# Router by ranks, squares summed by a product, and the first expert pair's rows selected on PE

## The chip, the core and the metric

The kernel runs on one core of a Trainium2 chip. The metric is device time in microseconds (us), the median over runs of one program. A run also gives a trace: what every engine did, how long, and what it waited for. Engines are PE (matmul), DVE (vector), ACT (activation), POOL and SP (here they only issue transfers); the data moves over 16 DMA engines.

## The reference

One step of a hybrid layer over 256 prompt tokens and 32 sample tokens, in float32. The stretch that matters here is the end of the layer: the residual stream, its norm, the router of the hierarchical mixture of experts, and the experts.

```python
h = x + mixed @ lw['w_o']
h = h + _hier_moe(_rmsnorm(h, lw['g_ffn']), lw)
...
g_idx = jnp.argmax(x @ w_grp + b_grp)                    # 1 group of 4
g_w   = softmax(g_logits)[g_idx]
top_v, top_i = lax.top_k(e_logits of that group, 2)      # 2 of its 4 experts
weights = g_w * softmax(top_v)
y = sum over experts of gate * (silu(x@w1) * (x@w3)) @ w2    # 16 experts, 2048 -> 512 -> 2048
```

Each of the 16 experts holds three matrices of 4 MB; all 201 MB are read once.

## The kernel before

**Stages.** Input projections, attention branches and merges run up to the product with `w_o`; then the router; then eight pairs of experts; then the last norm and the output. PE runs through all of it in program order, and so does each other engine; they meet at semaphores. There is no planner: the order is that of the code.

**The `w_o` loop** (PE L1107 to L1124). For each of 16 tiles `m` of 128 channels: a product of 16 matmuls into bank `m % 2` (L1113, waits for weight strips in a ring of four), then three transposes that bring tile `m` of the residual input `x` to channels-first (L1120), then `router(m - 1)` (L1088): logits of the tile before, accumulated in bank 2 (L1094), and its transposes to token rows (L1102, L1104). The residual input comes in four chunks (`x_chunk`, L1549) that ACT issues after a barrier of the engines (`phase_wait`), two at the start and two later; PE waits for a chunk by `xr_in`. A float32 matmul shows as two rows ("passes") in the trace, a transpose as one. ACT copies the transposed residual out of its bank (L1569), and DVE adds it to half the product (L2041), which gives `hTt`, tile `m` of h.

**The router** (DVE L2049 to L2128). ACT squares the token rows with a running sum (L1562), a product with a mask gathers the sample rows' sums over the four 32-row groups they are spread on (PE L1132), then mean, root, reciprocal, logits times scale plus bias (L2060). `first_max` (five short steps, L2069) is called three times: for the group, for the first and the second expert. From the one-hots come the assignment `AS`, its running counts per expert ("ranks", PE L1138 to L1141) and the gates. A token's rank is its slot (64 per expert). The largest count goes to `flag`, which each engine loads for a branch (`few_tokens`, L335); with at most 64 tokens per expert, as here, the engines take the branch described next.

**The pairs.** `pick(i)` (DVE L2162) builds a 0/1 matrix `sel` of tokens by 2x64 slots; `prepare(i)` (PE L1147) makes slot indices (L1151) and the transposed matrix (L1154) from it; `slots_of(i)` (DVE L2172) turns them into integers; POOL then gathers 128 rows of 8 KB of h by an indirect DMA from a copy in DRAM (L717) into `XGt`; PE transposes them (`gathered`, L1164) and DVE scales them into `XG` (`rows_in`, L2192). The up products of pair 0 and 7 run in eight steps (`up_fine`, L1183), each over one 2 MB slot of weights; the others in four steps of two slots (L1200). Then `down(i)`: transposes of the next pair's rows (`next_rows`, L1207, waits for its gather), transposes of the hidden layer (L1222), products with `w2` (L1233), and the scatter back to token rows (L1250). `prepare(i + 1)` stands early in the up products of pair `i`: in pair 0 after the second step (L1188).

**Weights.** Of 96 slots of 2 MB, nine fit on chip (`NSLOT`). Nine are loaded ahead; each later one is issued by SP when PE has finished with the slot's old content (L565: eight releases in the up products, two after the first half of `w2`, two after the second). So 87 fills follow the first release.

## Time and profile before

| | |
|---|---|
| median of 3 runs | 2096.85 us (2095.13 to 2097.07) |
| the profiled execution: time, and span of the trace | 2095.78 us, 2094.0 us |
| busy in the span: PE, DVE, ACT, POOL | 2019.7, 606.3, 257.6, 63.8 us |
| moved by DMA, mean rate | 404.31 MB, 193 GB/s |
| expert weights per slot | 2048 KB |

Times in rows are us from the start of the span. A matmul row's name ends with the tile (128*128) and the shape. Busy time says little here: PE is busy 96% of the span over stages with different limits. What counts is, stage by stage, what the last wait is for, and whether the DMA engines have work.

### The profile page before, as it was taken

Reading aid. Unit: us, or ns where it says so; the run is one execution under the profiler, and the core shown is the slowest. Engines: PE = TensorE matmul, PEld = TensorE weight load, DVE = VectorE, ACT = ScalarE, POOL = GpSimd, SP = SyncE. Lnnn points to the kernel's source line nnn. Section 1 sums busy time; section 2 is a strip of 40 time slices with the busy share of each in tenths; the row PEclk is TensorE's granted clock in tenths of the full one; section 3 lists DMA queues with packets and bytes.
Section 4 is the critical chain, followed back from the end, with each engine's and each line's share of the span. In section 5 each row is a group of like instructions: output and inputs, shape, how many; then the busy total and the mean of one; then the engine's idle time right before and its main releaser. Section 6 shows DMA issues by size and latency. Waiting matters only on the chain.

```text
span 2094.0 us, 26605 instructions
## 1 busy us (share of the span) xinstructions
PE 2019.7 (96%) x11213; PEld 1353.0 (65%) x11213; DVE 606.3 (29%) x1624; ACT 257.6 (12%) x619; POOL 63.8 (3%) x119
## 2 busy tenths in 40 slices
PE   7999999999999999999999999999996999989997
PEld 4767788777777777777777777777774333333332
DVE  3053222212212443534435345321003222121212
ACT  2121112122201010110101101000001000000002
POOL 0010000000000000000000000000000000000000
PEclk9999999999999999999999999999997999999999
DMA  9563434433234132431323313366433999999997
GB/s 300 93 194 122 134 125 149 158 129 119 86 121 148 59 125 73 135 114 54 125 92 116 125 42 123 119 219 223 153 130 131 422 428 426 428 427 427 428 423 277
DMA packets 196554, 404.31 MB, mean 193 GB/s; under 512 B 11632, under 2 KB 165968, under 8 KB 181328
## 3 DMA queue, kind: packets, MB, share of 16 engines
q1 hardware_dynamic: 187472, 379.37, 49.8%
q0 software_dynamic: 6304, 19.14, 3.3%
q10 hardware_dynamic: 2656, 4.06, 0.6%
q8 instruction: 90, 1.47, 0.3%
q14 instruction: 32, 0.26, 0.0%
HBM read 391.88 MB, written 10.67 MB: 192 GB/s over the span
## 4 chain that ended last, share of the span: by engine, by line
PE 88%; DMA 9%; DVE 1%; DVEq 1%; issue 0%; ACT 0%; SPq 0%; ACTq 0%
PE bank L766 21%; PE bank L970 19%; PE bank L972 6%; PE bank L1113 6%; PE bank L764 5%; PE bank L1200 5%; PE bank L1233 3%; PE bank L1080 3%; DMA Z<-in_w 3%; PE bank L1250 3%; DMA SC<-in_w 3%; PE bank L1183 2%; DMA ring<-in_w 2%; PE bank L1021 1%; PE bank L1015 1%; PE bank L743 1%
## 5 line engine op out<-in xcount | busy, mean ns | idle before, releaser
L766 PE MATMUL bank<-uT,ring 128*128 128x288 f32 (+2 forms) x1792 | 452.6, 409 | 0.6 <-DVE uT L1672 0.6
L970 PE MATMUL bank<-uT,ring 128*128 128x288 f32 x1536 | 408.1, 415 | 0.0
L766 PEld LDWEIGHTS bank<-uT,ring 128*128 128x128 f32 (+2 forms) x1792 | 332.1, 188 | 98.6 <-issue 7.8
L970 PEld LDWEIGHTS bank<-uT,ring 128*128 128x128 f32 x1536 | 283.6, 190 | 79.7 <-issue 3.1
L972 PE MATMUL bank<-Z,ring 128*128 128x288 f32 x512 | 140.5, 417 | 0.0
L1113 PE MATMUL bank<-SC,ring 128*128 128x288 f32 x512 | 128.4, 409 | 1.1 <-DVEq L355 1.1
L764 PE MATMUL bank<-ring,Z 128*128 128x256 f32 x512 | 117.4, 382 | 0.0
L1113 PEld LDWEIGHTS bank<-SC,ring 128*128 128x128 f32 x512 | 96.0, 190 | 29.6 <-DVEq L355 1.6
L1200 PE MATMUL bank<-ring,Z 128*64 128x512 f32 x352 | 104.5, 626 | 8.3 <-issue 8.3
L972 PEld LDWEIGHTS bank<-Z,ring 128*128 128x128 f32 x512 | 92.7, 189 | 25.6 <-issue 1.4
L764 PEld LDWEIGHTS bank<-ring,Z 128*128 128x128 f32 x512 | 95.4, 190 | 16.1 <-issue 3.7
L1522 ACT ACTIVATE Z<-bank 128x288 f32<-128x288 f32 x48 | 19.7, 411 | 589.5 <-PE bank L970 589.5
L1200 PE MATMUL bank<-Z 128*64 128x512 f32 x256 | 88.2, 609 | 4.1 <-issue 4.1
L2218 DVE TENSOR_TENSOR uT<-uT,bank 128x512 f32<-128x512 f32 x63 | 43.3, 688 | 115.3 <-PE bank L1250 115.3
L1200 PEld LDWEIGHTS bank<-ring,Z 128*64 128x64 f32 x352 | 32.9, 143 | 56.6 <-issue 56.5
L1200 PE MATMUL bank<-SC,Z 128*64 128x512 f32 x160 | 58.2, 608 | 5.6 <-issue 5.6
L1080 PE MATMUL bank<-Z,ring 128*128 128x288 f32 x256 | 62.3, 406 | 0.5 <-issue 0.5
L1080 PEld LDWEIGHTS bank<-Z,ring 128*128 128x128 f32 x256 | 48.6, 190 | 14.3 <-issue 1.0
L1250 PE MATMUL bank<-SC 128*128 128x512 f32 (+1 forms) x168 | 56.9, 601 | 0.0
L1200 PEld LDWEIGHTS bank<-Z 128*64 128x64 f32 x256 | 26.9, 140 | 41.2 <-issue 41.1
L1682 DVE TENSOR_TENSOR SC<-SC 128x287 f32<-128x287 f32 (+1 forms) x27 | 12.3, 457 | 138.5 <-ACT SC L1398 138.1
L2041 DVE SCALAR_TENSOR_TENSOR Z<-bank,Z 128x288 f32<-128x288 f32 x16 | 7.3, 457 | 141.1 <-ACT Z L1569 118.4
(408 smaller groups left out, 1931.2 us busy)
## 6 DMA issues: line engine op xcount, KB each, us to landing
ring<-in_w_in SPq DMA_DIRECT2D x102, 1024.0 KB, 7.8
ring<-in_w SPq DMA_DIRECT2D x40, 2048.0 KB, 31.4
Z<-in_w SPq DMA_DIRECT2D x31, 2048.0 KB, 30.4
SC<-in_w SPq DMA_DIRECT2D x21, 2048.0 KB, 29.1
ring<-in_w_mem_kv SPq DMA_DIRECT2D x16, 1024.0 KB, 7.7
ring<-in_w_o SPq DMA_DIRECT2D x16, 1024.0 KB, 7.7
ring<-in_p_b SPq DMA_DIRECT2D x8, 1024.0 KB, 5.3
ring<-in_p_m SPq DMA_DIRECT2D x8, 1024.0 KB, 8.0
```

Source lines behind the costliest of these rows:

```text
L743: ins = nc.tensor.transpose(bank[c % 8][:, t0:t0 + tn], X[0:tn, n, c * P:(c + 1) * P], ident[0:tn, 0:tn])
L764: ins = mm(bank[t][:, 0:STRIP], muT[:, c, P * t:P * t + P], rslot[q][:, c, :], start=c == 0, stop=c == KC - 1)
L766: ins = mm(bank[t][0:w, 0:T], rslot[q][:, c, w0:w0 + w], uT[:, c, :], start=c == 0, stop=c == KC - 1)
L970: ins = mm(b[:, 0:T], rslot[q][:, c, P * t:P * t + P], uT[:, c, :], start=c == 0, stop=c == last - 1)
L972: ins = mm(b[:, 0:T], rslot[q][:, k0 + c, P * t:P * t + P], Z[:, z0 + c, :], start=c == 0, stop=c == last - 1)
L1080: ins = mm(bank[n % 2][:, 0:T], wv[:, c, P * t:P * t + P], Z[:, Z_R + c, :], start=c == 0, stop=c == 7)
L1113: ins = mm(bank[m % 2][:, 0:T], rslot[(m // 2) % 4][:, c, P * (m % 2):P * (m % 2) + P], MX[:, c, :], start=c == 0, stop=c == KC - 1)
L1183: ins = mm(bank[2 + w][sides[x], :], XG[:, 4 * q + c, sides[x]], wv[:, x, c, :], start=q == 0 and c == 0, stop=q == 3 and c == 3)
L1200: ins = mm(bank[2 + w][sides[x], :], XG[:, 8 * h + c, sides[x]], wv[x][:, c, :], start=st < 2 and c == 0, stop=st >= 2 and c == 7)
L1233: ins = mm(bank[4 + b][sides[x], :], HS[:, 2 * h + c, sides[x]], wv[x][:, c, 512 * b:512 * b + 512], start=h == 0 and c == 0, stop=h == 1 ...
L1250: ins = mm(b[p0:p0 + tn, :], GP[:, i % 2, t0:t0 + tn], Yk[:, 512 * g:512 * g + 512], start=True, stop=True)
L2218: V.tensor_tensor(h, h, bank[SCB[n]][:, :], ALU.add).then_inc(s("sc_add"), 1)
```

## The change

In the `w_o` loop, the transposes of the residual tile (`residual`) stand one tile earlier: tile 0's ahead of the loop, tile `m + 1`'s behind the product of tile `m`. ACT squares each h tile channels-first (`tile_square`), DVE adds the squares of 15 tiles, and two products with a matrix of ones at the end put the sums of squares beside the logits, in rows 32 to 63 of bank 2. The sample tile's logits are brought to all four 32-row groups by four small products. DVE compares all logits of a group of four with each other at once; the number of larger ones is the rank within the group, from which `AS` follows. Softmax parts come after. PE gets small filler products (`keep_warm`). `pick` works in two steps over all slots instead of six. For pair 0 the rows are selected by products of h's token rows with `sel` (`own_rows`, 12 matmuls for each quarter, two quarters before and two within the up products) in place of the gather through DRAM; `prepare(0)` stands after the sixth up step and `prepare(1)` after the eighth.

```diff
-        lgT = cut(Z_t, 15104, T)[0:LOGITS, :]
+        lgT = cut(Z_t, 15104, T)[0:64, :]
+        h2sum = cut(Z_t, 12288, T)
+        h2one = cut(Z_t, 13952, T)
+        cmp_gt = cut(Z_t, 12800, 15, 16)
+        cmp_eq = cut(Z_t, 13040, 15, 16)
...
-            pload(NK_t[:, D + KC:D + KC + P + 3], a["const"][:, K_M32:NCALL], "nk_in")
+            pload(NK_t[:, D + KC:D + KC + P + 3], a["const"][:, K_M32:K_TOK + 3], "nk_in")
+            pload(TRI4, a["const"][:, K_TRI4:NCALL], "nk_in")
...
-                for i in range(EXPERTS // 2):
+                for i in range(1, EXPERTS // 2):
                     pool.wait_ge(s("idx_ev"), i + 1)
-                    if i:
+                    if i > 1:
                         pool.wait_ge(s("xgt_mm"), 4 * i)
...
                 mm(bank[2][0:LOGITS, 0:T], wr[:, m, :], h, start=m == 0, stop=m == KC - 1)
+                if m == KC - 1:
+                    pe.wait_ge(s("h2_add"), KC - 1)
+                    mm(bank[2][32:64, 0:T], ones[:, 0:32], h2sum, start=True, stop=False)
+                    pe.wait_ge(s("sq_done"), 14 + KC)
+                    mm(bank[2][32:64, 0:T], ones[:, 0:32], h2one, start=False, stop=True).then_inc(s("rt_mm"), 1)
...
+            def residual(m):
+
+                g = m // 4
+                pe.wait_ge(xr_in[g], 64)
+                if m >= 2:
+                    pe.wait_ge(s("xts"), m - 1)
+                for tt, (t0, tn) in enumerate(TOK):
+                    ins = nc.tensor.transpose(bank[4 + m % 2][:, t0:t0 + tn], XRC[g % 2][0:tn, tt, P * (m % 4):P * (m % 4) + P], ident[0:tn, 0:tn])
+                ins.then_inc(s("res_mm"), 1)
+
+            residual(0)
...
                 for c in range(KC):
                     ins = mm(bank[m % 2][:, 0:T], rslot[(m // 2) % 4][:, c, P * (m % 2):P * (m % 2) + P], MX[:, c, :], start=c == 0, stop=c == KC - 1)
                 ins.then_inc(s("wo_mm"), 1)
-                g = m // 4
-                pe.wait_ge(xr_in[g], 64)
-                if m >= 2:
-                    pe.wait_ge(s("xts"), m - 1)
-                for tt, (t0, tn) in enumerate(TOK):
-                    ins = nc.tensor.transpose(bank[4 + m % 2][:, t0:t0 + tn], XRC[g % 2][0:tn, tt, P * (m % 4):P * (m % 4) + P], ident[0:tn, 0:tn])
-                ins.then_inc(s("res_mm"), 1)
+                if m + 1 < KC:
+                    residual(m + 1)
...
-            pe.wait_ge(s("lg_ev"), 1)
-            pe.wait_ge(s("xts"), KC)
+            def keep_warm(n):
+
+                for _ in range(n):
+                    mm(bank[0][:, 0:P], ident, ident, start=True, stop=True)
+
+            pe.wait_ge(s("lg_ev"), 2)
+            for tt in range(2):
+                t0, tn = TOK[tt]
+                nc.tensor.transpose(bank[4][:, 64 * tt:64 * tt + 64], lgT[:, t0:t0 + tn], ident[0:64, 0:64])
+            for g in range(4):
+                ins = mm(bank[4][TS * g:TS * g + TS, P:P + 64], lgT[:, TP:T], ident[0:64, 0:64], start=True, stop=True)
+            ins.then_inc(s("rt_mm"), 1)
+            keep_warm(14)
+
+            pe.wait_ge(s("rt_a"), 1)
+            tri = CON[:, K_TRI:K_TRI + P]
+            for tt in range(3):
...
             for tt, (t0, tn) in enumerate(TOK):
-                ins = nc.tensor.transpose(bank[4][0:tn, 32 * tt:32 * tt + LOGITS], lgT[:, t0:t0 + tn], ident[0:LOGITS, 0:LOGITS])
-            pe.wait_ge(s("nk_in"), 96)
-            pe.wait_ge(s("sq_done"), 23)
-            mm(bank[5][:, 0:1], M32, ssq[:, 2, 0:1], start=True, stop=True).then_inc(s("rt_mm"), 1)
...
+                ins = mm(bank[1][:, 0:16], ones[0:tn, :], AS[0:tn, tt, :], start=tt == 0, stop=tt == 2)
             ins.then_inc(s("rank_mm"), 1)
+            keep_warm(4)
+
+            def own_rows(q):
+
+                for c in range(4):
+                    out = bank[4 + q % 2][:, P * c:P * c + P]
+                    for tt in range(2):
+                        mm(out, H[:, tt, 512 * q + c:512 * q + 512:4], sel[:, tt, :], start=tt == 0, stop=False)
+                    gs = slice(TS * q, TS * q + TS)
+                    ins = mm(out, H2[gs, c:512:4], sel[gs, 2, :], start=False, stop=True)
+                ins.then_inc(s("xgt_mm"), 1)
+
+            pe.wait_ge(s("tok_ev"), 9)
+            pe.wait_ge(s("sel_done"), 1)
+            own_rows(0)
+            own_rows(1)
             few = few_tokens(pe)
...
-                        if st == 1 and i + 1 < NPAIR:
-                            pe.wait_ge(s("xg_ev"), 4 * i + 4)
-                            prepare(i + 1)
+                        if i == 0 and st in (1, 3):
+                            pe.wait_ge(s("xg_ev"), st // 2 + 1)
+                            own_rows(2 + st // 2)
+                        if i == 0 and st == 5:
+                            prepare(0)
+                        if i == 0 and st == 7:
+                            pe.wait_ge(s("idx_ev"), 1)
+                            pe.wait_ge(s("gp_ev"), 1)
+                            prepare(1)
...
-                            pe.wait_ge(s("gath"), 16 * i + 32)
+                            pe.wait_ge(s("gath"), 16 * i + 16)
...
-                prepare(0)
-                pe.wait_ge(s("idx_ev"), 1)
-                pe.wait_ge(s("gp_ev"), 1)
-                pe.wait_ge(s("gath"), 16)
-                gathered(0, range(4))
...
+            def tile_square(m):
+
+                act.wait_ge(s("h_tile"), m + 1)
+                if m >= 2:
+                    act.wait_ge(s("h2_add"), m)
+                A(h2one if m else h2sum, hTt[:, m % 2, :], ACT.Square).then_inc(s("sq_done"), 1)
...
+                if m:
+                    tile_square(m - 1)
+            A(dummy[:, 0:1], vec["eps"][:, 0:1], ACT.Sqrt)
+            tile_square(KC - 1)
+            act.wait_ge(s("rt_mm"), 1)
+            A(lgT[32:64, :], bank[2][32:64, 0:T], ACT.Copy).then_inc(s("lg_ev"), 1)
             act.wait_ge(s("tail_mm"), KC)
-            A(lgT, bank[2][0:LOGITS, 0:T], ACT.Copy).then_inc(s("lg_ev"), 1)
-            for n in (3, 7, 8):
-                token_squares(False, n)
+            A(H[:, 0, 1536:2048], bank[3][:, :], ACT.Copy).then_inc(s("tok_ev"), 1)
             act.wait_ge(s("mean_sq"), 3)
             A(rst[:, 0:3], rsm[:, 0:3], ACT.Sqrt).then_inc(s("root"), 1)
+            A(H[:, 1, 1536:2048], bank[6][:, :], ACT.Copy).then_inc(s("tok_ev"), 1)
+            A(H2, bank[7][:, :], ACT.Copy).then_inc(s("tok_ev"), 1)
             A(dummy[:, 1:2], vec["eps"][:, 0:1], ACT.Exp)
...
+                if 2 <= m < KC:
+                    dve.wait_ge(s("sq_done"), 14 + m)
+                    V.tensor_tensor(h2sum, h2sum, h2one, ALU.add).then_inc(s("h2_add"), 1)
+                elif m == 1:
+                    dve.wait_ge(s("sq_done"), 15)
+                    dve.sem_inc(s("h2_add"), 1)
...
+            V.tensor_copy(lgT[0:LOGITS, :], bank[2][0:LOGITS, 0:T]).then_inc(s("lg_ev"), 1)
+            dve.wait_ge(s("rt_mm"), 2)
+            b4 = bank[4][:, 0:192].rearrange("p (t n) -> p t n", t=3)
+            V.tensor_scalar(rsm[:, 0:3], b4[:, :, 32:33].rearrange("p t a -> p (t a)"), 1.0 / D, EPS, ALU.mult, ALU.add).then_inc(s("mean_sq"), 1)
+            for tt in range(3):
+                V.scalar_tensor_tensor(lgt[:, tt, :], b4[:, tt, 0:LOGITS], rsm[:, tt:tt + 1], bias, ALU.mult, ALU.add)
+            dr()
+            fours = lgt.rearrange("p t (g x) -> p (t g) x", x=4)
+            rank, oh, top, dif, num = cut(RT, 60, 3, LOGITS), cut(RT, 120, 3, 4), cut(RT, 132, 15, 1), cut(RT, 148, 3, LOGITS), cut(RT, 208, 3, EXPERTS)
+            den, sumg = cut(RT, 368, 3, 1), cut(RT, 372, 3, 1)
+            other, own = fours.unsqueeze(2).to_broadcast([P, 15, 4, 4]), fours.unsqueeze(3).to_broadcast([P, 15, 4, 4])
+            gt4, eq4 = (b.rearrange("p g (x y) -> p g x y", x=4) for b in (cmp_gt, cmp_eq))
+            V.tensor_tensor(eq4, other, own, ALU.is_equal)
+            V.tensor_tensor(gt4, other, own, ALU.is_gt)
+            dr()
+            V.tensor_tensor(cmp_eq, cmp_eq, TRI4.unsqueeze(1).to_broadcast([P, 15, 16]), ALU.mult)
+            dr()
+            V.tensor_tensor(cmp_gt, cmp_gt, cmp_eq, ALU.add)
+            dr()
+            V.reduce_sum(rank.rearrange("p t n -> p (t n)"), cmp_gt.rearrange("p g (x y) -> p (g x) y", x=4), AX.X)
+            dr()
+            V.tensor_scalar(oh, rank[:, :, 0:4], 0.0, None, ALU.is_equal)
+            dr()
+            V.scalar_tensor_tensor(AS.rearrange("p t (g x) -> p t g x", x=4), rank[:, :, 4:LOGITS].rearrange("p t (g x) -> p t g x", x=4), 1.5,
+                                   oh.unsqueeze(3).to_broadcast([P, 3, 4, 4]), ALU.is_lt, ALU.mult)
+            dr()
+            dve.sem_inc(s("rt_a"), 1)
+            V.reduce_max(top.rearrange("p g a -> p (g a)"), fours, AX.X)
+            dr()
+            V.tensor_tensor(dif.rearrange("p t (g x) -> p (t g) x", x=4), fours, top.to_broadcast([P, 15, 4]), ALU.subtract)
+            dr()
+            dve.sem_inc(s("rt_a"), 1)
...
+            def pick(i):
+
+                one_hot = sel.rearrange("p t (x n) -> p t x n", x=2)
+                iota = CON[:, K_IOTA:K_IOTA + SLOTS].unsqueeze(1).unsqueeze(1).to_broadcast([P, 3, 2, SLOTS])
+                V.tensor_tensor(one_hot, iota, RK[:, :, 2 * i:2 * i + 2].unsqueeze(3).to_broadcast([P, 3, 2, SLOTS]), ALU.is_equal)
+                dr()
+                V.tensor_tensor(one_hot, one_hot, AS[:, :, 2 * i:2 * i + 2].unsqueeze(3).to_broadcast([P, 3, 2, SLOTS]), ALU.mult)
+                dr()
+                dve.sem_inc(s("sel_done"), 1)
+
+            def own_in(q):
+
+                dve.wait_ge(s("xgt_mm"), q + 1)
+                V.tensor_tensor(XG[:, 4 * q:4 * q + 4, :], bank[4 + q % 2][:, :].rearrange("p (a b) -> p a b", a=4),
+                                GV2[:, 4 * q:4 * q + 4].unsqueeze(2).to_broadcast([P, 4, P]), ALU.mult).then_inc(s("xg_ev"), 1)
+
+            dve.wait_ge(s("rank_mm"), 1)
+            V.tensor_copy(RK, bank[2][:, 0:48].rearrange("p (t n) -> p t n", t=3))
+            dr()
+            pick(0)
+            dve.wait_ge(s("rank_mm"), 2)
+            V.reduce_max(CNT[:, 0:1], bank[1][:, 0:16], AX.X)
+            dr()
+            V.tensor_copy(flag[:, :], CNT[:, 0:1]).then_inc(s("flag_done"), 1)
+
...
+            own_in(0)
+            own_in(1)
...
-                    if i:
-                        dve.wait_ge(s("gath"), 16 * i)
+                    if i > 1:
+                        dve.wait_ge(s("gath"), 16 * i - 16)
                     rs = slot_rs[:, i % 2:i % 2 + 1]
                     V.tensor_copy(slot_tok[:, :], bank[0][:, 0:1])
...
-                pick(0)
+                own_in(2)
+                own_in(3)
                 slots_of(0)
                 dve.wait_ge(s("gp_mm"), 1)
                 pick(1)
-                rows_in(0)
                 for i in range(EXPERTS // 2):
                     last = i + 1 == EXPERTS // 2```

On PE, at the head of the `w_o` loop (L1113 is the product of a tile, L1120 the residual's transposes, `xr_in0` the arrival of chunk 0, `phase_done` the barrier; L1080 belongs to the stage ahead), the order before:

```order
L1080 MATMUL bank<-Z,ring 128x288 x7
L1113 MATMUL bank<-SC,ring 128x288 [waits ring_full0,phase_done]
L1113 MATMUL bank<-SC,ring 128x288 x15
L1120 MATMUL bank<-CON,NK 128x128 [waits xr_in0]
L1120 MATMUL bank<-CON,NK 128x128
L1120 MATMUL bank<-CON,NK 128x32
L1113 MATMUL bank<-SC,ring 128x288 x16
```

and of the changed kernel, where the lines are L1137 (product) and L1127 (transposes):

```order
L1088 MATMUL bank<-Z,ring 128x288 x7
L1127 MATMUL bank<-CON,NK 128x128 [waits xr_in0,phase_done]
L1127 MATMUL bank<-CON,NK 128x128
L1127 MATMUL bank<-CON,NK 128x32
L1137 MATMUL bank<-SC,ring 128x288 [waits ring_full0]
L1137 MATMUL bank<-SC,ring 128x288 x15
L1127 MATMUL bank<-CON,NK 128x128 [waits xr_in0]
```

The wait for chunk 0 moved from behind the first product to ahead of it.

On PE in pair 0's up products (L1183), the order before, from the second step on (L1151 and L1154 are `prepare(1)`; `moe_full` is the arrival of a weight slot):

```order
L1183 MATMUL bank<-Z 64x512 [waits moe_full1]
L1183 MATMUL bank<-Z 64x512 x7
L1151 MATMUL bank<-Z,SC 128x18 [waits sel_done,xg_ev]
L1151 MATMUL bank<-Z,SC 128x18 x2
L1154 MATMUL bank<-CON,SC 128x128 x2
L1154 MATMUL bank<-CON,SC 128x32
L1183 MATMUL bank<-Z 64x512 [waits xg_ev,moe_full2]
```

and of the changed kernel, from the eighth step (L1230 is the up product, L1198 and L1201 `prepare(1)`, L1211 the transposes of pair 1's gathered rows):

```order
L1230 MATMUL bank<-ring,Z 64x512 [waits moe_full7]
L1230 MATMUL bank<-ring,Z 64x512 x7
L1198 MATMUL bank<-Z,SC 128x18 [waits sel_done,gp_ev,idx_ev]
L1198 MATMUL bank<-Z,SC 128x18 x2
L1201 MATMUL bank<-CON,SC 128x128 x2
L1201 MATMUL bank<-CON,SC 128x32
L1211 MATMUL bank<-CON,NK 128x128 [waits gath,gp_ev,idx_ev]
```

`prepare(1)`, on which pair 1's gather depends, moved from six steps ahead of the transposes of its rows to right in front of them.

## Rows read from the trace of the kernel before

**Rows 1.** Windows, two pairs: stretch, length, busy per engine, PEclk, DMA share, GB/s.

```profile
1617.50:1671.40 53.90, 53.90 (x248) 20.30 (x247) 12.35 (x26) 4.08 (x7) 1.00 (x1) 1.00 0.92 386
...
1941.00:1995.00 54.00, 48.77 (x211) 17.77 (x211) 8.95 (x17) 3.92 (x7) 0.94 (x1) 0.98 1.01 428
```

**Rows 2.** Chain that ended last, late pairs: start, length, what it was.

```profile
1980.66 30.49 DMA Z<-in_w
...
2056.48 16.65 DMA ring<-in_w
```

**Rows 3.** Timeline, head of the `w_o` loop: start, length, instruction, [idle before, releaser].

```profile
1394.61 35.81 PE L1080 MATMUL bank<-Z,ring 128*128 128x288 f32 x147
...
1431.52 0.47 ACTq L1552 DMA_DIRECT2D NK<-in_x_prompt  x1
...
1431.55 8.03 PE L1113 MATMUL bank<-SC,ring 128*128 128x288 f32 x32 [1.13 <-DVEq L355]
...
1440.77 0.61 PE L1120 MATMUL bank<-CON,NK 128*128 128x128 f32 x3 [1.20 <-DMA NK<-in_x_sample]
...
1441.32 8.03 PE L1113 MATMUL bank<-SC,ring 128*128 128x288 f32 x32
```

**Rows 4.** Windows around the router (PEclk is the third number from the end).

```profile
1588.00:1590.00 2.00, 0.01 (x1) 0.00 (x0) 1.28 (x3) 1.82 (x5) 1.18 (x2) 0.95 1.00 426
1590.00:1592.00 2.00, 0.56 (x2) 0.50 (x2) 0.55 (x3) 0.75 (x4) 1.55 (x4) 0.50 1.20 492
...
1600.00:1602.00 2.00, 1.97 (x12) 1.75 (x11) 0.05 (x1) 0.00 (x0) 0.00 (x0) 0.50 0.00 0
...
1614.00:1616.00 2.00, 2.00 (x9) 1.67 (x10) 0.72 (x2) 0.00 (x0) 0.00 (x0) 0.50 0.00 0
1616.00:1617.50 1.50, 1.50 (x10) 1.26 (x10) 1.13 (x2) 0.00 (x0) 0.00 (x0) 0.63 0.00 0
```

**Rows 5.** Chain from the last `w_o` products to the first expert product.

```profile
1584.39 0.39 PE bank L1120 x3
...
1598.47 0.61 PE bank L1139 x2
...
1600.47 1.51 PE bank L1141 x6
...
1602.68 0.55 DVEq L338
...
1603.69 0.32 DVE SC L2167
...
1607.74 6.11 DMA NK<-h_rows,slot_tok
...
1617.56 7.02 PE bank L1183 x32
```

**Rows 6.** Lines by form, 1430 to 1672: count, busy us, mean ns, idle before.

```profile
L2030 DVE TENSOR_TENSOR Z<-Z,VEC 128x320 f32<-128x320 f32 x1 | 0.5, 491 | 0.2 <-DVEq L355 0.2
...
L2073 DVE TENSOR_TENSOR Z<-Z 128x12 f32<-128x12 f32 x3 | 0.5, 171 | 0.2
```

**Rows 7.** Chain, pair 0 into pair 1.

```profile
1624.57 0.87 PE bank L1151 x6
...
1646.74 1.09 PE bank L1164 x8
...
1649.50 13.88 PE bank L1233 x64
1663.38 8.06 PE bank L1250 x24
```

**Rows 8.** Timeline of POOL and SP, pair 0: pair 1's gather, two weight fills.

```profile
1626.41 1.00 POOL L717 DMA_INDIRECT NK<-h_rows,slot_tok  x1 [17.65 <-DVEq L2185]
...
1656.56 1.19 SPq L534 DMA_DIRECT2D SC<-in_w  x2
```

**Rows 9.** View of tile NK, its gathers: from issue to landing.

```profile
DMA to landing us min/median/max: 6.1/13.3/13.5
```

More of the change, by code:

```diff
@@ L64 @@
 K_M32, K_TOK = 1344, 1472
-NCALL = 1475
+K_TRI4 = 1475
+NCALL = 1491
 BW = 640
@@ L1135, in _ @@
-            tri = CON[:, K_TRI:K_TRI + P]
-            for tt, (t0, tn) in enumerate(TOK):
-                for u in range(tt):
-                    mm(bank[6][0:tn, 16 * tt:16 * tt + 16], ones[:, 0:tn], AS[:, u, :], start=u == 0, stop=False)
-                mm(bank[6][0:tn, 16 * tt:16 * tt + 16], tri[0:tn, 0:tn], AS[0:tn, tt, :], start=tt == 0, stop=True)
-            for tt, (t0, tn) in enumerate(TOK):
-                ins = mm(bank[6][:, 48:64], ones[0:tn, :], AS[0:tn, tt, :], start=tt == 0, stop=tt == 2)
@@ new lines, in _ @@
+            ins.then_inc(s("rt_mm"), 1)
[3 more added lines that the diff above has]
+            for tt in range(3):
+                out = bank[2][:, 16 * tt:16 * tt + 16]
+                for u in range(tt):
+                    mm(out, ones, AS[:, u, :], start=u == 0, stop=False)
+                if tt < 2:
+                    mm(out, tri, AS[:, tt, :], start=tt == 0, stop=True)
+            for g in range(4):
+                gs = slice(TS * g, TS * g + TS)
+                ins = mm(bank[2][gs, 32:48], tri[0:TS, 0:TS], AS[0:TS, 2, :], start=False, stop=True)
@@ L2041, in _ @@
                 V.scalar_tensor_tensor(hTt[:, m % 2, :], bank[m % 2][:, 0:T], 0.5, xTs[:, m % 2, :], ALU.mult, ALU.add).then_inc(s("h_tile"), 1)
-                g = (m if m == KC - 1 else m - 1) // 4
-                if m == KC - 1 or (m and m % 4 == 0):
+                if 2 <= m < KC:
[4 more added lines that the diff above has]
+                    dve.sem_inc(s("h2_add"), 1)
+                g = (m - 1) // 4
+                if m and m % 4 == 0:
                     dve.wait_ge(s("tail_mm"), 4 * g + 4)
@@ L2056, in _ @@
             dr()
-            b4 = bank[4][:, 0:96].rearrange("p (t n) -> p t n", t=3)
             bias = VEC[:, N_VEC_IN - 24:N_VEC_IN - 4]
-            for tt, (t0, tn) in enumerate(TOK):
-                V.scalar_tensor_tensor(lgt[0:tn, tt, :], b4[0:tn, tt, 0:LOGITS], rsm[0:tn, tt:tt + 1], bias[0:tn, :], ALU.mult, ALU.add)
+            for tt in range(3):
+                V.scalar_tensor_tensor(lgt[:, tt, :], b4[:, tt, 0:LOGITS], rsm[:, tt:tt + 1], bias, ALU.mult, ALU.add)
+            dr()
@@ L2082, in _ @@
-            gl = lgt[:, :, 0:4]
-            first_max(oh, gl, gm)
-            V.tensor_tensor(ge, gl, gm.to_broadcast([P, 3, 4]), ALU.subtract)
-            el = lgt[:, :, 4:20]
-            for t in range(3):
-                V.tensor_tensor(big[:, t, :].rearrange("p (g x) -> p g x", g=4), el[:, t, :].rearrange("p (g x) -> p g x", g=4),
-                                oh[:, t, :].unsqueeze(2).to_broadcast([P, 4, 4]), ALU.mult)
-            dr()
-            V.reduce_sum(ei, big.rearrange("p t (g x) -> p t x g", g=4), AX.X)
@@ L2091, in _ @@
-            dr()
-            first_max(oh1, ei, m1)
-            V.scalar_tensor_tensor(e2, oh1, TAKEN, ei, ALU.mult, ALU.add)
-            dr()
-            first_max(oh2, e2, m2_)
-            V.tensor_tensor(m2_, m2_, m1, ALU.subtract)
-            dr()
-            dve.sem_inc(s("rt_a"), 1)
-            V.tensor_tensor(e2, oh1, oh2, ALU.add)
-            dr()
-            for t in range(3):
-                V.tensor_tensor(AS[:, t, :].rearrange("p (g x) -> p g x", g=4), oh[:, t, :].unsqueeze(2).to_broadcast([P, 4, 4]),
-                                e2[:, t, :].unsqueeze(1).to_broadcast([P, 4, 4]), ALU.mult)
@@ L2128, in _ @@
+            dr()
+            V.reciprocal(den, den)
+            dr()
+            V.tensor_tensor(RI[:, :, 2:18], num, den.to_broadcast([P, 3, EXPERTS]), ALU.mult)
+            dr()
+            own_in(0)
+            own_in(1)
             few = few_tokens(dve)
             def out_norm(tt):
-                dve.wait_ge(s("sq_done"), (30, 31, 32)[tt])
+                dve.wait_ge(s("sq_done"), (37, 38, 39)[tt])
                 if tt < 2:
```

105 lines of the change are left out of this document (29 added, 76 removed).

## The prediction, made before the changed kernel was run

> **What bounds the kernel now.** I read the end first. In the chain that ended last, the late pairs are waits for weights, up to the last one, which ends at 2073.1 [rows 2]. The windows by pair say why: 386 GB/s in the first pair's window, then 421 to 428, with a DMA share of 1.01, in each of the seven that follow up to 2049 (one stands here), while PE has gaps [rows 1]. By amount: 87 fills of 2.10 MB, seven gathers of 1.05 MB and some 0.8 MB of gains make 191 MB, at 428 GB/s 446 us, which is nearly all of the time between the first release of a slot (one up step after the first expert product, near 1621) and 2073. So from there on DMA sets the end: what starts the first release earlier is gained in full, what leaves the DMA engines without work later is lost in full. Ahead of that, PE's own order sets the time: the `w_o` loop, then a chain of short steps of 33.2 us, from the last `w_o` product's end at 1584.39 to the first expert product at 1617.56 [rows 5].
>
> So I price three things: the moved transposes ahead of the loop, the shorter chain, and what the new order in pair 0 does to the fills.
>
> **The `w_o` loop: +8.6 us, and +1.5 for the clock.** Before, PE starts the first product at 1431.55, and only its transposes wait for the residual's chunk 0, which lands at 1440.77, 9.2 us after ACT issued it; 8.03 us of product hide that, 1.20 us do not [rows 3]. Now the transposes stand first, with that wait, and the first product has to follow at 1441.32, where before the second one started. From there on the loop holds one product more (8.03) and, at the end of the last product, one group of transposes more (0.54): +8.57. Nothing gives it back, since PE is dense through the loop. The landing does not move: ACT issues behind the same barrier. PE is then idle for 10.3 us (1430.42 to 1440.77). In the router PE had nothing to do from 1588, and the granted clock was 0.50 (1.2 GHz) from 1590 on; when dense work came back at 1613.98, it was still 0.50 until 1616 and came to 1.00 near 1617.1, that is 3.1 us at half rate [rows 4]. The same here costs half of that, 1.5. Extra work in the loop (one square on ACT, one add on DVE per tile, under 0.5 us each) hides behind 9.6 us of PE per tile.
>
> **The chain: 33.2 becomes 20.0, -13.2 us.** Counted from the end of the last `w_o` product:
> - PE: `router(14)` 1.1, the last tile's logits 0.5, two products of squares with 288 columns at four passes of 0.25 (a product of 32 passes took 8.03 [rows 3]) 1.0: 2.6. The squares of tile 15 (DVE 0.5, ACT 0.4, DVE 0.5) are ready by 1.6. Transposes of tile 15 0.7, ten small passes for the logits 0.9: 4.2.
> - Mean, root, reciprocal with their hops 0.85, three scale-and-bias steps 0.55: 5.6.
> - DVE's steps have 240 elements now. 12 cost 171 ns and 320 cost 491 [rows 6], so 1.04 ns each and 408 ns for 240; with 0.07 of drain five of them, the first two overlapping, take 2.3, two small ones 0.5: `AS` at 8.4. Before it came at 14.1 (1598.47, [rows 5]).
> - Ranks: 18 passes. At full clock a pass with a 128-column weight load took 0.136 (1.09 for 8 [rows 7]): 2.4, to 10.8. Copy 0.25 and two `pick` steps of 384 elements at 0.56 and 0.07: 12.3.
> - `own_rows` 0 and 1: 24 passes each, at 0.136 to 0.145 (0.87 for 6 of L1151 [rows 7]) 3.4 each: 19.1. I count 0.9 for loading `flag` and the branch; DVE needed 1.0 (1602.68 to 1603.69 [rows 5]), and PE may hide all of it behind queued products. The first step starts at 20.0.
>
> What disappears is the selection on DVE, the gather with 6.11 us, and its 16 transposes at half clock. The scaling by `own_in` (0.7) lies beside `own_rows(1)`. This needs full clock all the way; the filler products cover the longest wait (4.2 to 8.4).
>
> **Pair 0: +18.2 us.** With t = 0 at the first up product, a step takes 3.51 (7.02 for two [rows 5]). `own_rows` 2 and 3 stand behind the second and fourth, `prepare(0)` (1.4) behind the sixth, so slots come free at 3.5, 7.0, 13.9, 17.4, 24.3, 27.9, 32.8 and 36.3. A fill flows 1.1 after its release and for 4.91 (2.10 MB at 428 GB/s): two gaps of 0.6, and the eight fills are through at 45.1, with pair 1's gather (2.5 of its own) at 47.5. But the gather is issued late: `prepare(1)` comes after the eighth step, its index product ends at 37.2 (0.87 [rows 7]), and POOL issues 1.0 later (1625.44 to 1626.41 [rows 7, 8]), at 38.2. Landing took 6.1 with nothing else moving and 13.3 with full queues [rows 9]; the queues are full at first and empty at the end, so I take 11.5: 49.7. Right behind `prepare(1)` PE stands at the transposes that wait for it, and behind them all of `down(0)`. Before, from these transposes to the next release it took 9.8 (1646.74 to 1656.56 [rows 7, 8]); 12 us of idle PE add 1.5 for the clock. So the next release is at 61.0 and flows at 62.1: 14.6 without work since 47.5. That release gives two slots (9.8), 6.9 later there are two more, and the next only after the scatter and a step, at 61.0 + 6.9 + 8.1 + 7.0 = 83.0: the DMA has run out at 81.7, 2.4 more. Later PE is ahead again. Sum 1.2 + 14.6 + 2.4 = 18.2. Before, `prepare(1)` ran at 1624.57 and its gather had 20 us of cover: the rows were there at 1646.74 with no wait.
>
> The Trainium skill (DMA: Bandwidth & Descriptors, section Queues, rings and completion order) says that each DMA engine takes turns between the queues that have work, a packet at a time. With even turns the gather would land some 8.6 after issue (an estimate: 1.05 MB at half of 428 GB/s, and the 3.65 that its 6.1 leaves over), and the sum would be 2.9 lower; the measured 13.3 says it gets about a quarter, so the measurement stands.
>
> **The sum.** 8.6 + 1.5 - 13.2 + 18.2 = +15.1 on the profiled execution's 2095.78: 2110.9, say 2111. That execution lies 1.1 below the median shown, well inside what I can tell. The bounds: `own_rows` passes between 0.11 (no weight load to wait for, 0.25 x 128/288) and 0.25 (half clock, 1.51 for 6 [rows 5]); flag 0 to 1.0; the gather 6.1 to 13.5 (-5.4, +2.0); the clock terms 0 to 1.5 each.
>
> **Rivals.**
> - *The clock falls in the router.* The rank products have 16 columns. In the trace PE was busy with such products for 1.97 of 2 us and stayed at 0.50 [rows 4]; if they count as little, the clock falls after the fillers too. Then 18 passes cost 2.2 more and 48 of `own_rows` 5: 2118. Against it: the fillers are 128 columns wide, and no gap exceeds 1 us. The Trainium skill (TensorE: Matmul & The Clock Gate, Part 1) says that sustained time, not the number of matmuls, releases the half rate; by that the forecast stands, and the row of 1600 doesn't bear it out.
> - *The gather lands early*, because the fills in front run out: 6.1 as in the quiet router. The wait shrinks by 5.4: 2105.5.
> - *The shortfall is made good* (the other side). If the fills were not at their ceiling, PE's stall in pair 0 would leave slots to be caught up with, and only the first three terms stay: 8.6 + 1.5 - 13.2 = -3.1, 2092.7, not slower. It decides if the rate after pair 0 exceeds some 445 GB/s. One 2 us window shows 492 [rows 4]; against it stand the flat 428 and the share of 1.01.
>
> **Numbers.** Forecast 0.56 (2106 to 2116), clock 0.16, early gather 0.17, made good 0.11. About 0.2% (4 us) is what a measurement here can tell from no change. The last case lies around that bound: 0.04 faster, 0.07 the same; the rest, 0.89, is slower. The range 2101 to 2121 leaves out that case and the far end of the clock's.
>
> **What would show it.** Right: PE idle some 10 us ahead of the first residual transposes near 1441, the last `w_o` product ending near 1594; the first up product 20 us behind it at clock 1.00; a PE wait of about 12 us for the gather between pair 0's up and down, with a hole in GB/s right behind it; then 428 to the end, the last landing near 2088. Wrong: a first up product before 1605 (chunk 0 earlier), no wait at the gather, a clock of 0.50 in `own_rows`, or windows above 440 GB/s after pair 0.

## The result, and the profile after

The changed kernel takes 2133.01 us (median of 5 runs, 2132.14 to 2133.99) against 2095.74 for the kernel before on the same chip: a ratio of 1.0178 [1.0164, 1.0192]. It is slower, as forecast, but by 37 us instead of 15; 2133 lies outside the range of 2101 to 2121. The profiled execution took 2132.14 with a span of 2130.3, 36.3 more than before.

I follow the prediction's three places in order. The head of the `w_o` loop, from the chain of the changed kernel that ended last (start, length, what it was):

```profile
1429.94 0.47 ACTq L1601
1430.44 7.82 DMA NK<-in_x_sample
1438.40 0.90 PE bank L1127 x3
1439.30 10.10 PE bank L1137 x32
```

The transposes (L1127) now wait for the residual's chunk, and the first product (L1137) takes 10.10 us where one at full clock takes 8.03 [rows 3]. The last `w_o` product ends at 1592.80, before at 1584.39. The barrier was 1.6 us earlier in this execution, so the stage is 10.0 longer. The sum is as predicted (+10.1), its parts are not: PE got the chunk 8.5 us after ACT's first issue instead of 9.2, and half clock cost some 2.4 (0.3 in the transposes, 2.1 in the product) instead of 1.5.

The chain from there to the first expert product, by the same view:

```profile
1592.80 0.59 PE bank L1102 x2
...
1600.30 0.39 PE bank L1166 x2
...
1603.72 1.03 PE bank L1181 x4
1604.75 0.76 PE bank L1183 x2
1605.52 1.23 PE bank L1181 x4
1606.75 0.76 PE bank L1183 x2
...
1619.47 5.67 PE bank L1230 x13
```

The ranks start 7.5 us behind the last product (predicted 8.4) and `own_rows` (L1181, L1183) 10.9 behind it (12.3): the router by ranks is faster than I reckoned. Then `own_rows` 0 and 1 take 15.75 together, 7.9 each, where 3.4 each were predicted: six passes take 1.79 to 1.99 us, or 0.30 to 0.33 a pass, not 0.136 to 0.145. The first expert product comes 26.7 behind the last `w_o` product; predicted were 20.0, before it was 33.2 [rows 5].

Pair 0, by the chain, up to pair 1's first step:

```profile
1629.00 1.13 PE bank L1181 x4
1630.13 0.66 PE bank L1183 x2
...
1636.36 9.62 PE bank L1230 x32
1645.98 1.13 PE bank L1181 x4
...
1653.33 9.67 PE bank L1230 x32
...
1671.43 0.89 PE bank L1198 x6
...
1673.27 11.50 DMA NK<-h_rows,slot_tok
1684.77 0.14 issue
1684.91 1.94 PE bank L1211 x8
...
2092.52 17.01 DMA ring<-in_w
```

`own_rows` 2 and 3 cost 7.36 each, and two up steps behind each take 9.62 and 9.67 where two took 7.02 [rows 5]. So `prepare(1)` (L1198) starts 52.0 behind the first up product, 15.7 later than the 36.3 that I put. Its gather lands 11.50 after POOL issued it, the 11.5 taken.

Windows of the changed kernel around `own_rows` and through pair 0 (length, busy time of PE, PEld, DVE, ACT and POOL; the last three numbers are PEclk, DMA share and GB/s; the windows of 5 us first, then those by stage):

```profile
1600.00:1605.00 5.00, 4.70 (x37) 4.37 (x38) 3.41 (x16) 1.74 (x3) 0.11 (x1) 0.90 0.98 378
1605.00:1610.00 5.00, 5.00 (x16) 3.88 (x16) 0.06 (x1) 0.00 (x0) 0.00 (x0) 0.50 0.36 143
1610.00:1615.00 5.00, 5.00 (x17) 3.88 (x16) 0.69 (x1) 0.00 (x0) 0.00 (x0) 0.50 0.00 0
1615.00:1620.00 5.00, 5.00 (x16) 3.58 (x17) 0.49 (x1) 0.00 (x0) 0.00 (x0) 0.50 0.02 3
...
1636.00:1643.00 7.00, 7.00 (x22) 2.15 (x23) 0.69 (x1) 0.00 (x0) 0.00 (x0) 0.60 0.18 75
1643.00:1653.00 10.00, 10.00 (x38) 6.85 (x34) 0.00 (x0) 0.00 (x0) 0.00 (x0) 0.94 0.96 369
1653.00:1660.00 7.00, 7.00 (x22) 2.17 (x23) 0.69 (x1) 0.00 (x0) 0.00 (x0) 0.60 0.18 75
...
1685.00:1697.50 12.50, 12.50 (x58) 6.79 (x60) 2.77 (x4) 0.60 (x1) 0.00 (x0) 0.83 0.06 12
```

The clock falls to 0.50 (1.2 GHz) and stays there while PE counts as busy all the time. (A busy PE here is one with a matmul in flight, and a product is longer in flight when its weights load longer: at least 392 ns in L1181, 275 in the same line with columns side by side, in e1_contig below.) Each slow `own_rows` also opens a hole in the fills (75 GB/s) that the prediction's 0.6 us gaps don't have; the hole at the gather (12 GB/s) is the one predicted. From 1760 on there is no more to catch up with: the later pairs run at 422 to 428, before at 421 to 428 (428 in [rows 1]), and the last weights land at 2109.5, where 2088 was forecast.

### The profile page after: what moved, and what is told of

Same layout as the page of the kernel before. It is cut to its first block, busy times and chain, and to the rows that moved or that the text cites. A ratio compares the mean times of both kernels' runs of the same rounds, so it can differ in the third digit from the quotient of the medians.

```text
span 2130.3 us, 26820 instructions
## 1 busy us (share of the span) xinstructions
PE 2059.3 (97%) x11344; PEld 1381.7 (65%) x11344; DVE 606.3 (28%) x1579; ACT 259.1 (12%) x619; POOL 64.8 (3%) x119
## 4 chain that ended last, share of the span: by engine, by line
PE 90%; DMA 7%; DVE 1%; issue 1%; DVEq 0%; SPq 0%; ACT 0%; ACTq 0%
PE bank L774 20%; PE bank L978 19%; PE bank L980 6%; PE bank L1137 6%; PE bank L1253 6%; PE bank L772 5%; DMA Z<-in_w 5%; PE bank L1286 4%; PE bank L1088 3%; PE bank L1230 3%; PE bank L1303 2%; PE bank L1029 1%; PE bank L1023 1%; PE bank L1181 1%; DMA ring<-in_w 1%
## 5 line engine op out<-in xcount | busy, mean ns | idle before, releaser
L1137 PE MATMUL bank<-SC,ring 128*128 128x288 f32 x512 | 130.6, 414 | 0.0
L1137 PEld LDWEIGHTS bank<-SC,ring 128*128 128x128 f32 x512 | 97.5, 193 | 28.7 <-issue 2.8
L1088 PE MATMUL bank<-Z,ring 128*128 128x288 f32 x256 | 62.3, 407 | 0.5 <-issue 0.5
L1088 PEld LDWEIGHTS bank<-Z,ring 128*128 128x128 f32 x256 | 48.6, 190 | 14.2 <-issue 1.0
```

Source lines behind the costliest of these rows:

```text
L1088: ins = mm(bank[n % 2][:, 0:T], wv[:, c, P * t:P * t + P], Z[:, Z_R + c, :], start=c == 0, stop=c == 7)
L1137: ins = mm(bank[m % 2][:, 0:T], rslot[(m // 2) % 4][:, c, P * (m % 2):P * (m % 2) + P], MX[:, c, :], start=c == 0, stop=c == KC - 1)
```

## Experiments

My theory after the two traces: `own_rows` is slow because its stationary columns lie 4 apart, and that slowness moves everything in pair 0. The rival: the clock falls in the thin router, and `own_rows` is slow for that reason alone. All edits are to the changed kernel unless another is named. The kernel before took 2096.1 to 2096.4 in these sessions.

**Columns side by side (e1_contig).**

```diff
-  mm(out, H[:, tt, 512 * q + c:512 * q + 512:4], ...)
+  mm(out, H[:, tt, 512 * q + P * c:512 * q + P * c + P], ...)   # the 32-row product alike
```

> The changed kernel, but own_rows takes its stationary columns side by side (step 1) and not every fourth one (step 4). The channels of pair 0's rows are then in another order than its weights, so pair 0's contribution isn't the reference's; amount and order of the work are the same. Theory A (the weight load with a column step of 4 is what makes a pass of own_rows last 0.28 to 0.31 us, and the slow passes let PE's clock fall): passes of 0.13 to 0.15, one own_rows 3.3 us in place of 7.4 to 7.9, clock 1.00 through pair 0's up steps, first up product 9 us earlier, first release 12 us earlier, holes in the fills behind the second and fourth step gone (each under 1 us): 2133 falls by 22 to 27, to 2106 to 2111. Rival B (a real float32 product with changing weights costs 0.28 whatever the step, or the 32-row group does): own_rows stays at 7 to 8 us, the time at 2133 within 2. Rival C (the clock falls by itself, since the products of own_rows count as little work): passes 0.14 at full clock but 0.25 soon after, up steps still at half rate, gain 8 to 12: 2121 to 2125.

Pair 0's channels don't match its weights here; the work is the same. 2116.92 (2113.7 to 2119.1), ratio 1.0093 [1.0076, 1.0109], 16.1 faster than the changed kernel, where theory A has 22 to 27. The weight loads of L1181 by line, after and then here (ns: min, median, max):

```profile
L1181 PEld LDWEIGHTS bank<-SC,uT x64: 307/329/331, 1603.5 to 1651.9; 128*128 128x128 f32 x64
```

```profile
L1181 PEld LDWEIGHTS bank<-SC,uT x64: 186/192/338, 1603.4 to 1641.2; 128*128 128x128 f32 x64
```

Its chain, the first of `own_rows(0)`, then two up steps and the start of `own_rows(2)`:

```profile
1603.71 0.74 PE bank L1181 x4
...
1618.28 8.28 PE bank L1230 x32
1626.56 0.64 PE bank L1181 x4
1627.20 0.41 PE bank L1183 x2
```

At full clock one `own_rows` takes 4.2. But the clock still falls at 1604, so `own_rows` 0 and 1 still take 7.1 and 7.5. The step is the larger part, not the whole.

**`prepare` earlier (e2_prep).** `own_rows(2)` and `(3)` stand behind the first and second up step, `prepare(0)` and `prepare(1)` behind the third and fourth.

```diff
-  if i == 0 and st in (1, 3): ... own_rows(2 + st // 2)
-  if i == 0 and st == 5: prepare(0)
-  if i == 0 and st == 7: ... prepare(1)
+  if i == 0 and st in (0, 1): ... own_rows(2 + st)
+  if i == 0 and st == 2: prepare(0)
+  if i == 0 and st == 3: ... prepare(1)
```

> The changed kernel, with own_rows 2 and 3 behind the first and second up step of pair 0, prepare(0) behind the third and prepare(1) behind the fourth (they stood behind the second, fourth, sixth and eighth). Theory A (the gather of pair 1 is issued too late, PE waits 12 us for it and the DMA engines then have nothing to do for 14 to 16): no wait at the transposes of pair 1's rows, the hole before the first release of pair 0's down goes, the time falls by 14 to 18: 2115 to 2119. Rival (the fills have slack that is used later, so the wait costs little): under 4 us, 2129 to 2133.

2121.01 (2120.2 to 2121.99), ratio 1.0116 [1.0099, 1.0133], 12.0 faster: less than expected. The gather now has cover (PE waits 0.2 for it instead of 12.1). From the first up product to the first product of `down(0)` it is 56.2 instead of 69.9, so 13.8 of the 14 to 18 are there; in the profiled execution the last `w_o` product ended 2.2 later than in the changed kernel. Each single step between two `own_rows` runs at half clock in part (5.9 to 6.2 instead of 3.5), but all eight together take 35.8 in both kernels, so this is not what is missing.

**Residual order as before (e3_res).** `residual(0)` behind the first `w_o` product again, tile 1's right after it.

```diff
-  residual(0)
   for m in range(KC):
       ... product m
+      if m == 0: residual(0)
       if m + 1 < KC: residual(m + 1)
```

> The changed kernel, with the transposes of residual tile 0 behind the first product of w_o again (tile 1 follows at once, the others stay one tile ahead). Theory A (the first product no longer covers the arrival of the residual's chunk 0): the wait of 9.6 falls to 1 to 2, the first product runs at full clock, everything behind comes 10 us earlier: 2121 to 2125. Rival (the fills that are loaded ahead end later and take the gain back): 2131 to 2134.

2123.10 (2121.3 to 2124.95), ratio 1.0129 [1.0112, 1.0146], 9.9 faster, as theory A has it. This is about the head's term, 8.6 + 1.5.

**All three (e4_all)**, with pair 0's weights loaded so that channels fit contiguous columns (the computation is whole again).

```diff
+  if i == 0: return a[...][0:2, 512 * q:512 * q + 512, :].rearrange("e (c p) n -> p e c n", c=4)
   (and the three edits above)
```

> All three edits in one kernel, with the computation whole: pair 0's up weights are loaded in the matching order of channels (runs of 2 KB in place of 8 KB, two transfers for each slot) and scaled by the gain vector in that order. Theory A, if the three parts add up (10 + 24 + 16): 2080 to 2086, faster than both kernels; the first up product some 15 us earlier than in the kernel before. Rival (the parts share one shortfall of the fills, and the sum is smaller): 2092 to 2105.

2095.10 (2088.14 to 2100.68, 10 runs), ratio 0.9996 [0.9982, 1.001]. The parts add: 16.1 + 12.0 + 9.9 = 38.0, measured 37.9. (That close is luck: counted from the kernel before of each session they are 16.8, 12.7 and 10.6, and 38.6 measured.) The 2080 to 2086 are missed because two of the three parts are smaller than put. `own_rows` 0 and 1 are still at half clock. The runs spread over 12 us, and those with the higher mean clock are the faster ones (2088.14 at 0.992, 2100.68 at 0.986).

**Denser filler (e5_dense)** on that kernel.

```diff
-  mm(bank[0][:, 0:P], ident, ident, ...)       # keep_warm(14), keep_warm(4)
+  mm(bank[0][:, :], ident, CON[:, 0:512], ...) # keep_warm(9), keep_warm(4)
```

> e4_all with denser filler: each filler product moves 512 columns (an estimate from the up steps' 0.228 us per such pass: 0.46 us a product) instead of 128, 9 ahead of the ranks (about 4.1 us, up to when AS is ready) and 4 behind them. In e4_all the granted clock fell to .50 at the end of the second filler and the first two own_rows took 7.4 us each instead of 4.2, the first two up steps 4.5 instead of 3.65. Theory (the idle and thin work before own_rows lets the clock fall; dense filler keeps it): clock 1.00 through the ranks, own_rows 0 and 1 at 4.2 each, first up product about 6.5 us earlier than in e4_all, 2086 to 2089 us, and runs that spread less than e4_all's 2088 to 2101. Rival (the clock falls there whatever runs on PE, as a rest after the dense w_o loop): own_rows still 7.4, 2093 to 2098.

2095.91 (2094.28 to 2096.82), ratio 0.9998 [0.9989, 1.0007]. The clock stays at 1.00 and `own_rows` take 4.2 each, but the filler is too long: the timeline has

```profile
1588.72 7.99 PE L1151 MATMUL bank<-CON 128*128 128x512 f32 x18
```

0.89 a product, twice what I reckoned from up steps, whose stationary side has 64 columns and whose two experts' products run side by side (16 passes of 0.59 each in 3.58). What the clock gave, the filler took. This filler does two things at once: its products are wider, and it also closes the 0.8 us for which PE stands idle ahead of the ranks in the changed kernel. Which of the two holds the clock no run here shows.

**Column step within one `own_rows` (e6_steps).** Its four products read columns 1, 2, 4 and 8 apart (the 32-row ones at most 4).

```diff
-  H[:, tt, 512 * q + c:512 * q + 512:4]
+  H[:, tt, at:at + P * by:by]   # by = 1, 2, 4, 8 for c = 0..3 in own_rows 2, 3
```

> after, but in own_rows 2 and 3 the four products of a tile read their stationary columns 1, 2, 4 and 8 apart (so pair 0's rows are wrong channels; own_rows 0 and 1 as in after). At one clock, side by side: theory (the weight load is what the step makes slow): step 1 as in e1_contig, 0.64 us for the 4 passes of the two 128-row products, step 4 as in after, 1.13; step 2 between them or at one of the two, step 8 (128-row products only, the 32-row product stays at 4) 1.13 or more; loads of 190 ns at step 1, over 300 at step 4. Rival (the step matters only by way of the clock): all four alike within 0.1 us.

One run (2128.09). `own_rows(2)` by the timeline, a 128-row and a 32-row row for each product, all at clock 1.00:

```profile
1629.06 0.71 PE L1184 MATMUL bank<-SC,uT 128*128 128x128 f32 x4
1629.70 0.48 PE L1186 MATMUL bank<-SC,uT 32*128 32x128 f32 x2
1630.12 0.74 PE L1184 MATMUL bank<-SC,uT 128*128 128x128 f32 x4
1630.78 0.50 PE L1186 MATMUL bank<-SC,uT 32*128 32x128 f32 x2
1631.21 1.20 PE L1184 MATMUL bank<-SC,uT 128*128 128x128 f32 x4
1632.34 0.73 PE L1186 MATMUL bank<-SC,uT 32*128 32x128 f32 x2
1633.00 1.22 PE L1184 MATMUL bank<-SC,uT 128*128 128x128 f32 x4
```

Steps of 1 and 2 cost the same (0.71, 0.74), 4 and 8 cost the same (1.20, 1.22), and `own_rows(3)` repeats all four: an edge between 8 and 16 bytes, not a price that grows. The Trainium skill (SBUF — State Buffer, section Door 1: The DMA port swizzle) says that SBUF is read in lines of 16 bytes and that two hits in a line are needed to hide its latency. The edge of these products agrees. Its figure that a stride of 4 float32 is still free does not: 4 apart cost 1.7 times as much here. This rule I had not weighed, and it speaks against the change.

**The router alone (e7_router).** No `own_rows`: pair 0's rows are gathered as before, `prepare(0)` follows the gates, eight up steps stand with nothing between but `prepare(1)` behind the second.

```diff
-  own_rows(0); own_rows(1)
+  prepare(0); pe.wait_ge(s("gath"), 16); gathered(0, range(4))
-  for i in range(1, EXPERTS // 2):   # POOL
+  for i in range(EXPERTS // 2):
```

> The change without own_rows: router by ranks, squares by the product, whole sample tile, residual order as in after; pair 0's rows are gathered as in before (prepare(0) once the gates are done, gather, transposes, then eight up steps without anything between, prepare(1) behind step 2). Theory (the router's half of the change saves 12.5 us of the chain after w_o, and the order in the w_o loop costs 10; everything after the first up step is as before): selection and gates ready 12.4 us after the last w_o product instead of 20.8, from there to the first up product 12.3 as in before, so first up 1617 and 2094 to 2096 us. Rival (the shorter chain meets the gather with rows not yet written or fills still on the queues, so the wait at the gather grows): 2098 to 2103.

2100.67 (2098.68 to 2103.87), ratio 1.0024 [1.0013, 1.0034]: the rival. Its chain:

```profile
1599.74 1.50 POOL h_rows L717 x3
1601.24 8.22 DMA h_rows<-uT
...
1611.13 5.89 DMA NK<-h_rows,slot_tok
...
1621.03 7.47 PE bank L1216 x32
```

The gather no longer waits for the selection but for h's last token rows, which are written to DRAM beside the prefetch of weights and land 8.2 us after POOL's issue, 15 behind the last product. In the kernel before the slower selection hid that. So the faster router alone gives less than the 12.5 expected as long as the rows go through DRAM (5.6 by the next experiment). `own_rows` reads them in SBUF and has no such wait.

**The router alone, residual order as before (e8_router_res).**

```diff
   (the edits of the router alone and of the residual order)
```

> e7_router with residual(0) behind the first w_o product, as in e3_res. Theory: the two parts add, first up about 1606.5, everything behind it 10 to 11 us earlier than in before: 2084 to 2087 us, the best so far. Rival (the gather now meets the prefetch of pair 0's weights, which in before ends about 1598, and lands later): 2088 to 2094.

2090.48 (2088.72 to 2091.44, 9 runs), ratio 0.9974 [0.9964, 0.9984]: 0.3% faster than the kernel before, short of the 2084 to 2087 for the same wait (h's last rows land 8.04 after their issue; the gather itself takes 5.99). The two parts add (10.2 between this kernel and the last).

**Less of the dense filler (e9_dense2)**, on the kernel with all three edits.

```diff
-  keep_warm(9) ... keep_warm(4)
+  keep_warm(5) ... keep_warm(1)
```

> e5_dense with fewer filler products: 5 ahead of the ranks and 1 behind them instead of 9 and 4. e5_dense showed a 512-column product at 0.89 us (18 passes, 7.99 us), twice what was reckoned with, so its filler ended 3.7 us after AS was ready and then 2.5 us after the selection. Theory (e5_dense kept the clock and lost the same time to too much filler): the clock stays at 1.00 with 4.4 and 0.9 us of it, own_rows 4.2 each, first up product 6 us earlier than e5_dense's 1610.6, 2088 to 2091 us. Rival (that little filler doesn't hold the clock through the ranks and the wait for the selection): own_rows 7.4 each, 2094 to 2097.

2090.59 (2087.98 to 2092.76, 8 runs), ratio 0.9971 [0.9961, 0.9982]. It beats both kernels, the one before by 0.3%, the changed one by 42 us. The first up product starts at 1605.7 by its chain, 11.9 earlier than before; some 8 of that are given back in the profiled execution, about what `own_rows` 2 and 3 (4.2 each) put between the releases, though no run separates this. It is level with e8_router_res (2090.48), which gathers pair 0's rows through DRAM: with all these edits the way over `own_rows` comes out the same as the gather.

**The filler alone (e10_after_dense)**, on the changed kernel.

```diff
   (the dense filler, keep_warm(5) and keep_warm(1); columns still 4 apart)
```

> after with that filler alone (5 and 1 products of 512 columns), columns still 4 apart. Theory A (the clock falls because of the thin stretch between w_o and own_rows): own_rows 0 and 1 at 7.4 each instead of 7.9 and up steps 1 and 2 in 7.0 instead of 9.5, 2129 to 2131 us. Theory B (own_rows with columns 4 apart lets the clock fall by itself, as own_rows 2 and 3 of after do): clock down within own_rows 0 or 1, first two up steps still over 9 us, 2131 to 2134.

2133.08 (2131.49 to 2134.51), ratio 1.0177 [1.0162, 1.0193]: no gain, theory B (its first two up steps take 8.2 though, not over 9). Its windows:

```profile
1605.00:1610.00 5.00, 5.00 (x17) 3.92 (x17) 1.81 (x9) 0.00 (x0) 0.00 (x0) 1.00 0.80 289
1610.00:1615.00 5.00, 5.00 (x17) 3.88 (x16) 0.69 (x1) 0.00 (x0) 0.00 (x0) 0.51 0.00 0
```

The clock holds into `own_rows(0)` and then falls, with PE busy for 5.00 of 5. So with columns 4 apart it falls in `own_rows` itself, though it came through the filler and the ranks; the next experiment differs in the column step alone.

**Contiguous columns and the filler (e11_contig_dense)**, which is what the prediction assumed.

```diff
   (the first edit and the dense filler, 5 and 1)
```

> e1_contig with that filler (pair 0's channels don't match its weights, as there): both conditions that the prediction took for own_rows, a pass at the price of a transpose and full clock. If the failed term is the whole of the miss, it must come out near the predicted 2111: own_rows 4.2 each (predicted 3.4), first up 6 to 7 us earlier than in e1_contig, 2109 to 2112 us. Rival (something else in pair 0 that the prediction left out): 2114 or more.

2112.10 (2110.47 to 2114.17), ratio 1.0078 [1.0063, 1.0093]; the prediction's time was 2111. The same windows:

```profile
1605.00:1610.00 5.00, 5.00 (x30) 3.82 (x29) 0.92 (x3) 0.00 (x0) 0.00 (x0) 1.00 0.38 152
1610.00:1615.00 5.00, 5.00 (x27) 2.68 (x28) 0.69 (x1) 0.00 (x0) 0.00 (x0) 1.00 0.01 3
```

All four `own_rows` run at clock 1.00 and take 4.2 each, not the 3.4 predicted. That is 3.2 more in all, and the chain ahead of them is some 2 faster than put, so the forecast's sum comes to about 2112. The four kernels make a table of two by two: with columns 4 apart the filler gives nothing (2133.0, 2133.1), with contiguous ones 4.8 (2116.9, 2112.1; runs of one kernel spread over up to 5). `own_rows` 0 and 1 need both: they take 7.9 each in the changed kernel, 7.1 and 7.5 with the step alone mended, 7.4 and 8.0 with the filler alone, 4.2 with both.

## Why the prediction was wrong

The direction and three of its steps hold.
- *The `w_o` loop:* +10.1 predicted, +10.0 in the trace, 9.9 by the experiment that undoes it. The mechanism is right; that the sum fits so well is luck, since the chunk came 0.8 sooner and half clock cost 0.9 more than put.
- *The chain up to the selection:* 12.3 predicted, 10.9 measured, and nothing of the 0.9 for the flag is seen (the up step follows `own_rows` at once).
- *The gather:* issued behind the eighth step, 11.5 to land, PE waiting for it (12.1), a hole right behind. The exact 11.5 is luck: it was chosen between 6.1 and 13.3, and the same gather took 13.0 in e1_contig and 12.0 in e11_contig_dense.

**The step that failed is the price of `own_rows`: "24 passes each, at 0.136 to 0.145", 3.4 each, with "full clock all the way".** A pass cost 0.30 at full clock (1.13 and 0.66 for six) and 0.33 at half. I took the price from L1164 and L1151 [rows 7]. L1164 is of the same tile shape, and its stationary columns are even 4 or 8 apart, but it is a transpose, and I did not hold it against other transposes. The trace of before has them, with contiguous columns (L1102) and with columns 2 apart (L1222):

```profile
L1102 PEld LDWEIGHTS bank<-CON,Z x32: 138/140/143, 1450.3 to 1586.5; 128*128 128x128 f32 x32
L1164 PEld LDWEIGHTS bank<-CON,NK x128: 185/196/230, 1614.0 to 2002.8; 128*128 128x128 f32 x128
L1222 PEld LDWEIGHTS bank<-CON,SC x28: 194/209/219, 1647.6 to 2001.7; 128*128 128x128 f32 x28
```

By these rows a transpose pays for columns apart too: 140 ns contiguous, 196 to 209 apart, at 2 already (no run changes the step of a transpose alone). What hid it is that such a load is about as long as that of a product with contiguous columns (192 in e1_contig), so L1164 and L1151, a product of contiguous columns, agreed at 0.136 and 0.145. No row of before had a float32 product with its columns apart at full clock, and I did not bound that case. The upper bound of 0.25 that I gave stands for the clock alone, and even that is below the 0.30. A smaller part of the term was off as well: with columns side by side and at full clock `own_rows` still costs 4.2, since PE's loads pause at each change between 128-row and 32-row products (see the last section).

The miss by its parts, in the trace: ahead of the first up product `own_rows` 0 and 1 cost 9.0 more than put, less the 2.3 that the chain was faster, +6.7. In pair 0 `own_rows` 2 and 3 cost 7.9 more and the six up steps at a falling clock 7.8 more, together the 15.7 by which `prepare(1)` is late. That is 22.4, and the measured difference stands 22 above the forecast's +15.1. All of the 15.7 reached the end: the first up product is 1.9 later than before and the last weights land 36.4 later, which leaves 34.5 for pair 0, 18.2 + 15.7 and 0.6. PE's lateness in pair 0 is late fills, and the fills are at their ceiling later.

*The rivals.* The clock did fall, with a chance of 0.16. But its time, 2118, has passes at half clock and no slower weight load, and its reason, the thin rank products, is one of two: in e1_contig, whose `own_rows` keeps the clock once it has it, it falls at 1604 as in the changed kernel, and with the filler alone (e10_after_dense) it holds through the ranks and falls in `own_rows`. The Trainium skill (TensorE: Matmul & The Clock Gate, Part 1) says that sustained time releases the half rate. If the profile's busy time is what counts, the trace does not agree: PE was busy for 5.00 of 5 us in each window from 1605 to 1620 and stayed at 0.50. But that busy time holds the weight loads (PEld 3.58 to 3.88 of the 5), so this alone does not refute the page. Why the clock falls in products that wait for their weight loads is argued from these rows, and not shown by itself. The gather did not land early. The shortfall was not made good: no slice of the page behind pair 0 exceeds 428.

## What to carry to other kernels

Price a PE step from a row of the same kind of instruction and the same access, not of the same tile shape: a transpose has its own price and its own price for columns apart. For the stationary operand of a float32 product keep the columns at most 2 apart, and lay out the weights' channels to suit, which cost nothing that shows here (the three edits of e4_all add up with it). Where a chain is made shorter, look for what it hid: the rows' way through DRAM came up behind the faster selection. And price the new way against the old one with both at their best: the gather that `own_rows` replaced was no slower (2090.48 against 2090.59).
